# Routing of the expert layers: look-up in PSUM, exponential on VectorE, ScalarE loop of eight tiles

## The chip, the cores and the metric

The kernel runs on one core of a Trainium2 chip. Its engines are TensorE (PE in the rows, its weight loads PEld), VectorE (DVE), ScalarE (ACT), GpSimd (POOL) and SyncE (SP), which issues the DMAs. The metric is the device time of one execution in microseconds.

## The reference

256 tokens of width 1024 pass a two-layer block (gated linear attention, then sliding-window attention) and a second block with a mixture of experts. Each of the first two layers ends in `peer`, product-key retrieval over 128 x 128 experts of one neuron each, and only that is touched here:

```
s1, s2  = scores of the two query halves against 128 subkeys each, for 8 heads
v1, i1  = top_k(s1, 16);  v2, i2 = top_k(s2, 16)
cand    = v1[..., :, None] + v2[..., None, :]            # 16 x 16 sums
cs, ci  = top_k(cand, 16)
e       = take(i1, ci // 16) * 128 + take(i2, ci % 16)   # the expert picked
g       = softmax(cs)
a       = gelu(x . u_tab[e]);   y = sum over picks of g * a * v_tab[e]
```

## The kernel before

The kernel doesn't gather experts. It multiplies all tokens by the whole first table (`peer_u`, 16384 rows), keeps the GELU of every product in `W`, builds from the picks a table of gates by one-hot products, multiplies `W` by it, and multiplies the result by the whole second table. All of it is in fp32: each table tile of 128 x 1024 is split in a high and a low part, and each product is three matmuls (high x high, high x low, low x high).

The first-table stage has 128 tiles per layer. A tile is two halves of 512 columns, and there are four half buffers `w_parts`. For each half:

- SyncE loads the tile to one of four `ring` slots when TensorE has begun a later tile (`ring_free`).
- ScalarE copies the half to its high part (`high`, L1404) when TensorE has released the buffer (`half_free`).
- GpSimd subtracts it from the tile to get the low part (L2460).
- TensorE issues 12 matmuls of 256 columns (L952), so 24 per tile, into bank 0, 1, 2 or 3.
- After the second half ScalarE stores the GELU of the bank in `W` (`gelu`, L1409).

Each engine's program is written out in order. The loops are hardware loops (`Fori`). ScalarE's loop before the change holds four tiles, in the order `high(i+2)`, `gelu(i)`, and it runs in three parts: tiles 0 to 35, 36 to 71, 72 to 123. At the start of the second and the third part ScalarE takes one exponential (L1421) that VectorE has asked for (`cs`) and answers by `ecs`.

Beside this stage VectorE does the routing (`peer_dve`), for two token tiles of 128 tokens one after the other (the loop over `a`): top 16 of each score row (MAX8, FIND_INDEX8, MATCH_REPLACE8, L1964 to L1977), the 16 x 16 sums (L1989), their top 16 (L1996 to L2009), then the look-up. That compares the rank of each pick with 0 to 15 (L2031), multiplies by the indices (L2034) and adds up (L2037), each on 2048 columns in SBUF, once for each query half. Last come the sum of the exponentials and the division (L2040 to L2044), for which VectorE waits for ScalarE's exponential.

When tile 71 is done, TensorE turns the picks of the two token tiles with three transposes each (L905). They need a bank of 0 to 3, so TensorE waits first for the GELU of tile 71 (`gelu`) and for `picked`. VectorE copies each turned tile to `route` (L2050). TensorE starts tile 72, and ScalarE its third part, when both copies are done; the arena of `W` from tile 72 on lies over the routing's buffers.

## Time and profile before

| what | us |
|---|---|
| median of three runs | 3252.25 (3243.31 to 3254.04) |
| the profiled execution | 3245.69 |
| its span | 3243.9 |
| TensorE busy | 2985.8 (92%) |
| VectorE busy | 1982.0 (61%) |
| ScalarE busy | 1762.6 (54%) |
| GpSimd busy | 1583.7 (49%) |

The span is from the first to the last instruction that was profiled. Busy shares are means over stages that are bound by different engines. In the chain of waits that ended last TensorE has 66% of the span, and ScalarE, GpSimd and VectorE have 9%, 8% and 6%. Matmul ends are modelled, so a matmul of 256 columns is shown with 0.28 us though the next one starts 0.12 us later.

### The profile page before, as it was taken

To read this page: it belongs to the slowest core of one execution; us is meant where nothing else is said; L and a number is where in the kernel's file an instruction comes from. 1 tells how busy PE (TensorE), PEld (TensorE's weight loads), DVE (VectorE), ACT (ScalarE), POOL (GpSimd) and SP (SyncE) were. 2 spreads that over 40 slices of the span, in tenths; PEclk is the share of its full clock that TensorE was granted. 3 is DMA by queue.
4 is the path that set the end of the run, shared out by engine and by line. 5 is a ranking of instruction groups with operands and counts; after the bars stand their busy time and mean duration, and the time that the engine had idled before them with its cause. 6 is when DMAs were issued, how large, how long until landed. Compare 5 with 4: busy or idle time off the path is not lost.

```text
span 3243.9 us, 57950 instructions
## 1 busy us (share of the span) xinstructions
PE 2985.8 (92%) x18908; PEld 2694.4 (83%) x18908; DVE 1982.0 (61%) x3234; ACT 1762.6 (54%) x3309; POOL 1583.7 (49%) x1229
## 2 busy tenths in 40 slices
PE   7988999987999986999999789999889999999998
PEld 6678999976787875899999667888789789999997
DVE  6647370047888868272600678888684436777776
ACT  1124777788555553367767875555554315555554
POOL 5867998875444436149988645444261011000100
PEclk8989999999999997999999989999999999999998
DMA  6544555520766643345555127666464235555553
GB/s 250 200 154 166 170 170 166 183 94 32 257 228 226 229 143 118 100 161 169 168 168 181 52 84 255 233 229 214 138 220 158 95 117 190 193 191 191 200 192 125
DMA packets 153461, 552.55 MB, mean 170 GB/s; under 512 B 16896, under 2 KB 19712, under 8 KB 153232
## 3 DMA queue, kind: packets, MB, share of 16 engines
q1 hardware_dynamic: 151136, 547.42, 49.8%
q10 hardware_dynamic: 2224, 3.87, 0.4%
q8 instruction: 53, 0.87, 0.1%
q14 instruction: 48, 0.39, 0.0%
HBM read 550.17 MB, written 1.05 MB: 170 GB/s over the span
## 4 chain that ended last, share of the span: by engine, by line
PE 66%; issue 9%; ACT 9%; POOL 8%; DVE 6%; DMA 1%; ACTq 0%; POOLq 0%; DVEq 0%; SPq 0%
PE bank L978 20%; PE bank L952 15%; PE bank L1223 11%; PE bank L747 6%; PE bank L1244 5%; ACT hT L1444 5%; POOL w_parts L2460 5%; PE bank L695 3%; ACT hT L1440 2%; POOL arena L2504 1%; DVE w_parts L1756 1%; POOL arena L2506 1%; POOL arena L2508 1%; DMA arena<-stream 1%; DMA ring<-stream 0%
## 5 line engine op out<-in xcount | busy, mean ns | idle before, releaser
L2460 POOL TENSOR_TENSOR w_parts<-ring,w_parts 128x512 fp32r<-128x512 f32 x512 | 686.0, 1366 | 180.1 <-ACT w_parts L1404 175.3
L952 PE MATMUL bank<-h_parts,w_parts 128*128 128x256 f32 x6144 | 745.6, 284 | 25.3 <-POOL w_parts L2460 23.3
L952 PEld LDWEIGHTS bank<-h_parts,w_parts 128*128 128x128 f32 x6144 | 741.3, 193 | 29.7 <-POOL w_parts L2460 27.2
L2504 POOL TENSOR_TENSOR arena<-arena,cact 128x1024 f32<-128x1024 f32 x80 | 166.9, 2086 | 742.0 <-DMA arena<-stream 741.9
L1404 ACT ACTIVATE w_parts<-ring 128x512 fp32r<-128x512 f32 x512 | 321.5, 630 | 204.1 <-PE bank L952 200.0
L1596 ACT ACTIVATE w_parts<-ring 128x512 fp32r<-128x512 f32 x384 | 242.0, 631 | 266.0 <-PE bank L1223 168.5
L1223 PEld LDWEIGHTS bank<-h_parts,w_parts 128*128 128x128 f32 x3072 | 374.2, 193 | 3.8 <-DVE arena L2322 1.5
L1223 PE MATMUL bank<-h_parts,w_parts 128*128 128x256 f32 x3072 | 375.1, 284 | 1.4 <-DVE arena L2322 1.4
L978 PE MATMUL bank<-w_parts,a_parts 128*128 128x512 f32 x1536 | 370.8, 397 | 1.2 <-DVE a_parts L2107 1.2
L978 PE MATMUL bank<-h_parts,a_parts 128*128 128x512 f32 x1536 | 365.0, 393 | 6.0 <-DVE a_parts L2107 5.9
L2391 DVE TENSOR_TENSOR w_parts<-ring,w_parts 128x512 fp32r<-128x512 f32 x376 | 271.1, 732 | 149.0 <-ACT w_parts L1596 145.7
L978 PEld LDWEIGHTS bank<-h_parts,a_parts 128*128 128x128 f32 x1536 | 284.9, 188 | 79.0 <-DVE a_parts L2107 20.8
L978 PEld LDWEIGHTS bank<-w_parts,a_parts 128*128 128x128 f32 x1536 | 286.8, 190 | 60.3 <-DVE a_parts L2107 2.0
L1463 ACT ACTIVATE a_parts<-arena 128x256 fp32r (+1 forms) x256 | 107.1, 418 | 363.9 <-PE bank L978 362.0
L695 PE MATMUL bank<-h_parts,w_parts 128*128 128x256 f32 x1920 | 240.6, 287 | 15.2 <-DVE w_parts L1756 13.2
L695 PEld LDWEIGHTS bank<-h_parts,w_parts 128*128 128x128 f32 x1920 | 236.3, 195 | 18.9 <-issue 14.6
L2107 DVE TENSOR_TENSOR a_parts<-arena,a_parts 128x256 fp32r<-128x256 f32 x256 | 164.9, 644 | 123.2 <-ACT a_parts L1463 123.0
L1756 DVE TENSOR_TENSOR w_parts<-ring,w_parts 128x512 fp32r<-128x512 f32 x184 | 196.5, 1100 | 60.8 <-ACT w_parts L1297 59.5
L926 PE MATMUL bank<-hT,h_parts 128*128 128x128 f32 x1024 | 146.0, 295 | 68.8 <-ACT hT L1444 66.2
L2065 DVE COPY bank<-cst 128x128 f32<-128x128 f32 x2 | 0.6, 295 | 326.8 <-ACT arena L1409 326.8
L926 PEld LDWEIGHTS bank<-hT,h_parts 128*128 128x128 f32 x1024 | 129.1, 202 | 85.7 <-ACT hT L1444 85.4
L1244 PE MATMUL bank<-w_parts,a_parts 128*128 128x512 f32 x768 | 182.1, 393 | 6.0 <-DVE a_parts L2403 5.1
(325 smaller groups left out, 4661.7 us busy)
## 6 DMA issues: line engine op xcount, KB each, us to landing
ring<-stream SPq DMA_DIRECT2D x786, 512.0 KB, 3.4
arena<-stream SPq DMA_DIRECT2D x192, 512.0 KB, 4.3
hT<-stream SPq DMA_DIRECT2D x32, 512.0 KB, 4.6
mean<-stream SPq DMA_DIRECT2D x32, 512.0 KB, 4.6
arena<-consts ACTq DMA_DIRECT2D x1, 1536.0 KB, 6.9
xT<-xin ACTq DMA_DIRECT2D x1, 1024.0 KB, 10.8
out<-hT SPq DMA_DIRECT2D x4, 256.0 KB, 2.2
arena<-subk ACTq DMA_DIRECT2D x2, 128.0 KB, 2.2
```

Of the source, the lines that this page charges most:

```text
L695: mm = pe.matmul(t[:, 0:T], w[:, wp, q * P:(q + 1) * P], h_parts[:, hp, 4 * j + q, :], start=(j == 0 and q == 0 and i == 0), stop=(j == 1 ...
L926: mm = pe.matmul(bank[4 + k][:, (s % 4) * P:(s % 4 + 1) * P], hot2[:, s, :].bitcast(F32), hot1[:, s, :], start=True, stop=True)
L952: mm = pe.matmul(bank[k][:, 0:T], w[:, wp, ws], h_parts[:, hp, 4 * j + q, :], start=(j == 0 and q == 0 and i == 0), stop=(j == 1 and q == ...
L978: mm = pe.matmul(bank[4 + 2 * a + e][:, :], a_parts[:, k % 2, ap, a * P:(a + 1) * P], w[:, wp, :], start=False, stop=False, skip_group_che ...
L1223: mm = pe.matmul(bank[2 * e_par + m][:, f * T:(f + 1) * T], w[:, wp, q * P:(q + 1) * P], h_parts[:, hp, 4 * j + q, :], start=(j == 0 and q ...
L1244: mm = pe.matmul(bank[4 + 2 * a + e][:, :], a_parts[:, ap, f, a * P:(a + 1) * P], w[:, wp, :], start=(f == 0 and i == 0), stop=(f == 1 and ...
L1404: act.activation(w_parts[half % HALVES][:, 0, :], ring[slot_][:, j * 512:(j + 1) * 512], ACT.Copy).then_inc(sem(f"{n}_high"), 1)
L1596: act.activation(w_parts[half % HALVES][:, 0, :], ring[s][:, j * 512:(j + 1) * 512], ACT.Copy).then_inc(sem("e_high"), 1)
L1756: dve.tensor_tensor(w[:, 1, :], slot(name, k)[:, j * 512:(j + 1) * 512], w[:, 0, :].bitcast(F32), ALU.subtract).then_inc(sem("x_low"), 1)
L2391: dve.tensor_tensor(w[:, 1, :], ring[moe_slot(k)[0]][:, j * 512:(j + 1) * 512], w[:, 0, :].bitcast(F32), ALU.subtract).then_inc(sem("e_low ...
L2460: pool.tensor_tensor(w[:, 1, :], ring[(base + k) % RING][:, j * 512:(j + 1) * 512], w[:, 0, :].bitcast(F32), ALU.subtract).then_inc(sem(f" ...
L2504: pool.tensor_tensor(b3, b3, c_b, ALU.mult).then_inc(sem("mod_step"), 1)
```

## The change

It touches the first-table stage of both `peer` layers.

- VectorE's look-up works on 512 columns (two heads) at a time, in the PSUM banks 4, 5 and 6, which no matmul uses in this stage. The numbers 0 to 15 and a copy of the top values (`values_p`) lie in bank 7, so that each two-input operation of the sums and of the look-up reads one input from PSUM and one from SBUF.
- The exponential is made by VectorE with `exp_dve`, a series of order 8, on 128 columns in SBUF. The semaphores `cs` and `ecs` are gone, and VectorE does both token tiles without waiting for ScalarE.
- The picks are turned in banks 4 and 5. TensorE waits for `picked` alone, and goes on to tile 72 without waiting for VectorE's copies. ScalarE's second part waits for `picked` alone too.
- ScalarE's loop holds eight tiles, in the order `gelu(i)`, `high(i+3)`, with three `high` ahead of it. It has two parts, tiles 0 to 71 and 72 to 119, and eight tiles behind them.

```
-            pe.wait_ge(sem(f"{n}_gelu"), ROUTE_TILE)
+            pe.wait_ge(sem(f"{n}_picked"), TT)
             for a in range(TT):
-                ... wait for picked, open a tile of banks 0 to 3, wait till it is free
                 for k in range(3):
-                    mm = pe.transpose(t[:, k * P:(k + 1) * P], R.pick[:, a, k, :], ident)
-                mm.then_inc(full_sem(f"{n}_rt{a}"), 1)
-            for a in range(TT):
-                pe.wait_ge(free_sem(f"{n}_rt{a}"), freed(f"{n}_rt{a}"))
+                    mm = pe.transpose(bank[4 + a][:, k * P:(k + 1) * P], R.pick[:, a, k, :], ident)
+                mm.then_inc(sem(f"{n}_turned"), 1)
...
-            for i in range(2):
+            for i in range(3):
                 high(i, 2 * i, tile_at(i), base)
-            for part, (first, last) in enumerate(((0, 36), (36, 72), (72, NK - 4))):
-                ... from the second part on: wait for cs, Exp, then ecs
-                with act.Fori(first // 4, last // 4) as it:
-                    for k in range(4):
-                        high((k + 2) % 4, ...)
-                        gelu(bass.ds(it * 4 + k, 1), k, ...)
+            for first, last in ((0, ROUTE_TILE), (ROUTE_TILE, NK - 8)):
+                if first:
+                    act.wait_ge(sem(f"{n}_picked"), TT)
+                with act.Fori(first // 8, last // 8) as it:
+                    for k in range(8):
+                        gelu(bass.ds(it * 8 + k, 1), k % 4, it * 16 + 2 * (k + 1))
+                        high((k + 3) % 8, it * 16 + 2 * (k + 3), it * 32 + tile_at(k + 3), base)
...
+                dve.tensor_copy(values_p, v)
                 dve.tensor_tensor(c4, v4[:, :, 0, :]...,
-                                             v4[:, :, 1, :]..., ALU.add)
+                                             p4[:, :, 1, :]..., ALU.add)
...
+                dve.tensor_scalar(cs, cs, -87.0, None, ALU.max)
+                exp_dve(dve, weights, cs, R.ca, R.cb)
...
+                for f, rank in enumerate((R.caf, R.cbf)):
+                    for i in range(PH // 2):
+                        wide = bank[4 + i % 3][:, :]
+                        dve.tensor_tensor(w4, rank3[...], iota16[...], ALU.is_equal)
+                        dve.tensor_tensor(w4, w4, i4[:, hs, f, :]..., ALU.mult)
+                        dve.tensor_reduce(R.pick[:, a, f, ...], wide..., AX.X, ALU.add)
-                dve.wait_ge(sem(f"{n}_ecs"), a + 1)
```

`exp_dve(dst, x, tmp, tmp2)` was there and is called anew. Each line below waits for the one before it:

```
k = tensor_scalar(x * 1/ln2)        # rounded to int, in tmp
tmp2 = tensor_copy(k)
x = scalar_tensor_tensor(tmp2 * -LN2_HI + x);  x = scalar_tensor_tensor(tmp2 * -LN2_LO + x)
k = tensor_scalar(tmp2 + 127);  k = tensor_scalar(k << 23)
dst = tensor_scalar(x * c[8])
for i in 7..1: dst = scalar_tensor_tensor((dst + c[i]) * x)
dst = scalar_tensor_tensor((dst + 1) * tmp)
```

ScalarE, the start of the first loop of the stage, before. `arena<-bank` is a GELU, `w_parts<-ring` half a `high`, ISA and REGISTER_ALU handle waits and counts.

```order
L1403 ISA
L1404 ACT_TABLE_LOAD
L1404 ACTIVATE w_parts<-ring 128x512
L1403 REGISTER_ALU
L1404 ACTIVATE w_parts<-ring 128x512
L1409 ISA
L1409 ACT_TABLE_LOAD
L1409 ACTIVATE arena<-bank 128x256
L1399 REGISTER_ALU
L1403 REGISTER_ALU
L1404 ACTIVATE w_parts<-ring 128x512
L1403 REGISTER_ALU
```

And of the changed kernel:

```order
L1404 ISA
L1404 ACT_TABLE_LOAD
L1404 ACTIVATE arena<-bank 128x256
L1394 ISA
L1398 REGISTER_ALU
L1399 ACTIVATE w_parts<-ring 128x512
L1398 REGISTER_ALU
L1399 ACTIVATE w_parts<-ring 128x512
L1404 ISA
L1404 ACTIVATE arena<-bank 128x256
L1398 REGISTER_ALU
L1399 ACTIVATE w_parts<-ring 128x512
```

Before, the body of four tiles has two table loads, one for each kind of activation; now the body of eight tiles has one, ahead of the first GELU, and the second loop has none.

TensorE, the end of tile 71 and the turn, before, with the semaphores that a row waits for:

```order
L942 COMPARE_AND_BRANCH
L905 MATMUL bank<-cst,arena 128x128 [waits bank_free3,p0_picked,p0_gelu]
L905 MATMUL bank<-cst,arena 128x128 x2
L905 MATMUL bank<-cst,arena 128x128 [waits bank_free0,p0_picked]
L905 MATMUL bank<-cst,arena 128x128 x2
L942 UNCONDITIONAL_BRANCH [waits bank_free0,bank_free3]
L942 ISA
L952 MATMUL bank<-h_parts,w_parts 128x256 [waits p0_low]
```

And of the changed kernel:

```order
L937 COMPARE_AND_BRANCH
L902 MATMUL bank<-cst,arena 128x128 [waits p0_picked]
L902 MATMUL bank<-cst,arena 128x128 x5
L937 UNCONDITIONAL_BRANCH
L937 ISA
L947 MATMUL bank<-h_parts,w_parts 128x256 [waits p0_low]
```

The waits for `gelu`, for free banks between the transposes, and on the branch into the next loop are gone; the six transposes stand in one row.

VectorE, the look-up of a token tile and what closes it, before:

```order
L2025 CAST arena<-arena 128x128
L2031 TENSOR_TENSOR arena<-arena,cst 128x2048
L2034 TENSOR_TENSOR arena<-arena 128x2048
L2037 TENSOR_REDUCE arena<-arena 128x128
L2031 TENSOR_TENSOR arena<-arena,cst 128x2048
L2034 TENSOR_TENSOR arena<-arena 128x2048
L2037 TENSOR_REDUCE arena<-arena 128x128
L2040 TENSOR_REDUCE arena<-arena 128x8
L2042 RECIPROCAL arena<-arena 128x8
```

Of the changed kernel, first what is new ahead of it (L1841 to L1861 are `exp_dve`):

```order
L2014 TENSOR_SCALAR arena<-arena 128x128
L1841 TENSOR_SCALAR arena<-arena 128x128
L1843 CAST arena<-arena 128x128
L1845 SCALAR_TENSOR_TENSOR arena<-arena 128x128
L1847 SCALAR_TENSOR_TENSOR arena<-arena 128x128
L1849 TENSOR_SCALAR arena<-arena 128x128
L1851 TENSOR_SCALAR arena<-arena 128x128
L1856 TENSOR_SCALAR arena<-arena 128x128
L1859 SCALAR_TENSOR_TENSOR arena<-arena 128x128 x7
```

then the first two of the eight rounds of the look-up:

```order
L2024 CAST arena<-arena 128x128
L2032 TENSOR_TENSOR bank<-arena,bank 128x512
L2036 TENSOR_TENSOR bank<-bank,arena 128x512
L2039 TENSOR_REDUCE arena<-bank 128x32
L2032 TENSOR_TENSOR bank<-arena,bank 128x512
L2036 TENSOR_TENSOR bank<-bank,arena 128x512
L2039 TENSOR_REDUCE arena<-bank 128x32
```

The two rounds of three operations on 2048 columns in SBUF have become eight rounds of three on 512 columns with PSUM operands, and 16 operations on 128 columns have come in ahead of them.

## Rows read from the trace of the kernel before

**Rows 1.** The page's costliest groups: shape, count, busy us, mean ns, idle before

```profile
L2460 POOL TENSOR_TENSOR w_parts<-ring,w_parts 128x512 fp32r<-128x512 f32 x512 | 686.0, 1366 | 180.1 <-ACT w_parts L1404 175.3
L952 PE MATMUL bank<-h_parts,w_parts 128*128 128x256 f32 x6144 | 745.6, 284 | 25.3 <-POOL w_parts L2460 23.3
```

**Rows 2.** Windows view, both first-table stages: length, busy us (count), clock, DMA

```profile
302.70:689.50 386.80, 373.74 (x3078) 371.33 (x3078) 117.88 (x366) 276.39 (x446) 343.60 (x257) 1.00 0.53 174
1419.20:1806.10 386.90, 373.64 (x3078) 371.12 (x3078) 118.13 (x368) 276.37 (x446) 342.97 (x257) 1.00 0.53 174
```

**Rows 3.** Windows view, a stretch without VectorE work

```profile
530.00:689.00 159.00, 159.00 (x1326) 159.00 (x1326) 0.00 (x0) 114.95 (x188) 138.64 (x110) 1.00 0.56 182
```

**Rows 4.** Timeline of ScalarE, one loop turn: start, us, engine, line

```profile
369.62 1.28 ACT L1409 ACT_TABLE_LOAD   x1
381.14 1.28 ACT L1409 ACT_TABLE_LOAD   x1
```

**Rows 5.** Waits of TensorE, 302.7:510 and 1419.2:1630: total us, times, longest

```profile
PE bank L952 <- POOL w_parts L2460: 11.6, 9, 2.5
...
PE bank L952 <- POOL w_parts L2460: 11.8, 10, 2.5
```

**Rows 6.** L2460 on GpSimd in 302.7:315.2, 347.8:355, 334:340: ns min/median/max

```profile
L2460 POOL TENSOR_TENSOR w_parts<-ring,w_parts x11: 1293/1302/1308, 302.6 to 315.2; 128x512 fp32r<-128x512 f32 x11
...
L2460 POOL TENSOR_TENSOR w_parts<-ring,w_parts x4: 1286/2304/3312, 346.6 to 352.4; 128x512 fp32r<-128x512 f32 x4
...
L2460 POOL TENSOR_TENSOR w_parts<-ring,w_parts x5: 1292/1294/1342, 333.1 to 338.2; 128x512 fp32r<-128x512 f32 x5
```

**Rows 7.** Timeline, first look-up of layer 0 (start us, us, instruction, idle before)

```profile
339.90 2.29 DVE L2031 TENSOR_TENSOR arena<-arena,cst 128x2048 f32<-128x2048 f32 x1
...
342.23 3.27 DVE L2034 TENSOR_TENSOR arena<-arena 128x2048 f32<-128x2048 f32 x1
...
345.53 2.29 DVE L2037 TENSOR_REDUCE arena<-arena 128x128 f32<-128x2048 f32 x1
...
346.67 2.54 PE L952 MATMUL bank<-h_parts,w_parts 128*128 128x256 f32 x19 [1.57 <-POOL w_parts L2460]
```

**Rows 8.** Timeline, 128-column VectorE operations beside GpSimd

```profile
334.43 1.34 DVE L2015 TENSOR_TENSOR arena<-arena 128x128 f32<-128x128 f32 x1
...
335.80 1.20 DVE L2019 TENSOR_SCALAR arena<-arena 128x128 uint32<-128x128 uint32 x1
```

**Rows 9.** L2470 on GpSimd and L2072 on VectorE, whole program: ns min/median/max

```profile
L2470 POOL TENSOR_TENSOR hT<-cst,mean x128: 1039/1042/1044, 687.9 to 1907.2; 128x512 f32<-128x512 f32 x128
...
L2072 DVE TENSOR_TENSOR h_parts<-bank,mean x128: 680/683/692, 690.8 to 1907.8; 128x512 fp32r<-128x512 f32 x128
```

**Rows 10.** Timeline, the turn after tile 71 of layer 0

```profile
522.59 0.55 PE L905 MATMUL bank<-cst,arena 128*128 128x128 f32 x3 [0.99 <-ACT arena L1409]
...
524.81 0.29 DVE L2044 TENSOR_TENSOR arena<-arena 128x128 f32<-128x128 f32 x1
...
525.16 0.55 PE L905 MATMUL bank<-cst,arena 128*128 128x128 f32 x3 [2.03 <-DVE arena L2044]
...
526.68 1.28 ACT L1404 ACT_TABLE_LOAD   x1 [2.53 <-DVE mean L2050]
...
526.70 1.14 PE L952 MATMUL bank<-h_parts,w_parts 128*128 128x256 f32 x4 [1.00 <-DVE mean L2050]
```

**Rows 11.** Windows view of L952, just behind the turn (PE, PEld, PEclk, DMA)

```profile
526.70:530.00 3.30, 3.30 (x16) 3.30 (x17) 0.52 0.50 160
```

**Rows 12.** Timeline of VectorE: ends of the two token tiles, layer 0

```profile
292.73 0.49 DVE L1964 MAX8 arena<-arena 128x8 f32<-128x128 f32 x2 [1.37 <-ACT arena L1343]
...
354.57 2.29 DVE L2037 TENSOR_REDUCE arena<-arena 128x128 f32<-128x2048 f32 x1
414.80 0.29 DVE L2040 TENSOR_REDUCE arena<-arena 128x8 f32<-128x128 f32 x1 [57.94 <-ACT arena L1421]
...
475.56 2.29 DVE L2037 TENSOR_REDUCE arena<-arena 128x128 f32<-128x2048 f32 x1
```

More of the change, by code:

```diff
@@ L1412, in tile_at @@
                 return 16 * ((base + i) // RING + 1)
-            for i in range(2):
+            for i in range(3):
                 high(i, 2 * i, tile_at(i), base)
-            for part, (first, last) in enumerate(((0, ROUTE_TILE // 2), (ROUTE_TILE // 2, ROUTE_TILE), (ROUTE_TILE, NK - 4))):
-                if part:
-                    act.wait_ge(sem(f"{n}_cs"), part)
-                    act.activation(R.cs, R.cs, ACT.Exp).then_inc(sem(f"{n}_ecs"), 1)
-                if part == 2:
-                    for a in range(TT):
-                        act.wait_ge(free_sem(f"{n}_rt{a}"), freed(f"{n}_rt{a}"))
-                with act.Fori(first // 4, last // 4) as it:
-                    for k in range(4):
-                        high((k + 2) % 4, it * 8 + 2 * (k + 2), it * 16 + tile_at(k + 2), base)
-                        gelu(bass.ds(it * 4 + k, 1), k, it * 8 + 2 * (k + 1))
-            for i in range(NK - 4, NK):
-                if i + 2 < NK:
-                    high((i + 2) % 4, 2 * (i + 2), tile_at(i + 2), base)
+            for first, last in ((0, ROUTE_TILE), (ROUTE_TILE, NK - 8)):
[5 more added lines that the diff above has]
+                        high((k + 3) % 8, it * 16 + 2 * (k + 3), it * 32 + tile_at(k + 3), base)
+            for i in range(NK - 8, NK):
                 gelu(slice(i, i + 1), i % 4, 2 * (i + 1))
+                if i + 3 < NK:
+                    high((i + 3) % 8, 2 * (i + 3), tile_at(i + 3), base)
             act.wait_ge(sem(f"{n}_negated"), 1)
@@ L2015, in peer_dve @@
                 dve.tensor_tensor(R.cs, R.cs, R.sum[:, 0:8].unsqueeze(2).broadcast_to([P, PH, TOPK]),
-                                            ALU.subtract).then_inc(signal(f"{n}_cs"), 1)
-                dve.wait_ge(sem(f"{n}_cs"), signalled(f"{n}_cs"))
+                                            ALU.subtract).then_inc(signal("dve_step"), 1)
+                dve.wait_ge(sem("dve_step"), signalled("dve_step"))
+                weights = R.pick[:, a, 2, :]
+                cs = R.cs.rearrange("p h k -> p (h k)")
+                dve.tensor_scalar(cs, cs, -87.0, None, ALU.max).then_inc(signal("dve_step"), 1)
+                dve.wait_ge(sem("dve_step"), signalled("dve_step"))
+                exp_dve(dve, weights, cs, R.ca, R.cb)
                 cif = R.ci.rearrange("p h k -> p (h k)").bitcast(U32)
@@ L2039, in peer_dve @@
-                dve.wait_ge(sem(f"{n}_ecs"), a + 1)
-                dve.tensor_reduce(R.sum[:, 0:8], R.cs, AX.X, ALU.add).then_inc(signal("dve_step"), 1)
+                for f, rank in enumerate((R.caf, R.cbf)):
+                    rank3 = rank.rearrange("p (h k) -> p h k", h=PH)
+                    for i in range(PH // 2):
+                        hs = slice(2 * i, 2 * i + 2)
+                        wide = bank[4 + i % 3][:, :]
+                        w4 = wide.rearrange("p (h k x) -> p h k x", h=2, k=TOPK)
+                        dve.tensor_tensor(w4, rank3[:, hs, :].unsqueeze(3).broadcast_to([P, 2, TOPK, TOPK]),
+                                          iota16.unsqueeze(1).unsqueeze(1).broadcast_to([P, 2, TOPK, TOPK]), ALU.is_equal)\
+                           .then_inc(signal("dve_step"), 1)
+                        dve.wait_ge(sem("dve_step"), signalled("dve_step"))
+                        dve.tensor_tensor(w4, w4, i4[:, hs, f, :].unsqueeze(2).broadcast_to([P, 2, TOPK, TOPK]), ALU.mult)\
+                           .then_inc(signal("dve_step"), 1)
+                        dve.wait_ge(sem("dve_step"), signalled("dve_step"))
+                        dve.tensor_reduce(R.pick[:, a, f, 2 * i * TOPK:(2 * i + 2) * TOPK],
+                                          wide.rearrange("p (k x) -> p k x", x=TOPK), AX.X, ALU.add).then_inc(signal("dve_step"), 1)
+                        dve.wait_ge(sem("dve_step"), signalled("dve_step"))
@@ L2041, in peer_dve @@
+                w3 = weights.rearrange("p (h k) -> p h k", h=PH)
+                dve.tensor_reduce(R.sum[:, 0:8], w3, AX.X, ALU.add).then_inc(signal("dve_step"), 1)
                 dve.wait_ge(sem("dve_step"), signalled("dve_step"))
@@ L2461, in peer_pool @@
                                            w[:, 0, :].bitcast(F32), ALU.subtract).then_inc(sem(f"{n}_low"), 1)
-            for a in range(TT):
-                pool.wait_ge(free_sem(f"{n}_rt{a}"), freed(f"{n}_rt{a}"))
+            pool.wait_ge(sem(f"{n}_route"), TT)
             with pool.Fori(0, T // TURN) as it:
```

35 lines of the change are left out of this document (12 added, 23 removed).

## The prediction

> **What bounds the kernel now.** I read the page first. The costliest group on GpSimd and the costliest on TensorE belong to one stage, the first-table stage, and each waits for the other's chain: TensorE lost 23.3 us to GpSimd there [rows 1]. So the windows view comes next. Each of the two stages takes 386.8 to 386.9 us [rows 2]. A stretch without VectorE work shows what it could take: TensorE is busy without a gap, 1326 matmuls in 159.00 us, 0.12 us each [rows 3], and ScalarE's table load comes again after 11.52 us per four tiles [rows 4], which is 96 x 0.12. So 128 tiles at TensorE's own pace are 32 x 11.52 = 368.6 us, and each stage loses 18.2 us. Two table loads per four tiles are already inside this pace: they cost TensorE nothing while GpSimd is undisturbed.
>
> The waits view gives the largest part: TensorE waited 11.6 us for L2460 in layer 0 before the turn, 11.8 us in layer 1 [rows 5]. Why, the durations of L2460 tell: 1.30 us undisturbed, up to 3.31 us beside the look-up [rows 6]. The timeline says beside which operations: the two-input ones on 2048 columns in SBUF (L2031, L2034), which take 2.29 us, or 3.3 us when they have first to wait for GpSimd. Behind L2034 TensorE stood 1.57 us [rows 7]. L2037, a reduction with one input, takes 2.29 us at any time. So VectorE and GpSimd keep each other out of SBUF when VectorE reads two inputs there.
>
> The rest is the turn after tile 71. The last matmul of the tile, shown as 0.28 us, starts 0.99 + 0.28 us ahead of 522.59, at 521.32, and the first of tile 72 at 526.70 [rows 10]. At full pace it would have come 0.12 us later, so 5.3 us are lost: waits of 0.99, 2.03 and 1.00 us and two times three transposes. Then 16 matmuls took 3.30 us where 27.5 would have fitted, at a granted clock of 0.52, the lower of its two levels, after TensorE had stood nearly still [rows 11]: 11.5 x 0.12 = 1.4 us. 11.6 + 5.3 + 1.4 = 18.3 us, which closes with 18.2.
>
> **Part by part.** *The look-up and the sums in PSUM.* The trace of before has this form of operation beside GpSimd in the next stage: L2072 reads one input from PSUM and one from SBUF, 512 columns, and takes 0.680 to 0.692 us in 128 cases, while GpSimd's L2470, which runs beside it, takes 1.039 to 1.044 us in all 128 [rows 9]. Neither touches the other. So L2460 stays at 1.30 us and the waits of rows 5 go: 11.6 + 11.8 = 23.4 us. The bounds are 23.4 gained and, if a PSUM operand did not help, a loss that the second rival works out. I take 23.4, since rows 9 is the same form at the same width. For VectorE a look-up is then 16 x 0.68 plus 8 reductions of a quarter of 2.29, or 15.5 us, near what it took.
>
> *The exponential on VectorE.* 16 new operations on 128 columns in SBUF per token tile. Beside GpSimd such operations took 1.34 and 1.20 us [rows 8], alone 0.29 (L2044 in rows 10): they wait for the end of a GpSimd operation. I take 1.25 us, so 20 us per token tile. What they do to GpSimd is in the third of rows 6: five L2460 beside them took 1.292 to 1.342 us. Two of at most 1.34 us are 2.68 us per tile, and TensorE needs 2.88 us for a tile, so it stays ahead. Cost 0. The other bound: each keeps GpSimd out for its own 0.29 us, 4.6 us per token tile, of which GpSimd's spare time in 20 us (7 tiles x 0.28) takes 2.0. That leaves 2.6 us, four times 10.4 us in the program.
>
> The Trainium skill speaks against this part: "SBUF — State Buffer", section "Who interferes with whom", says that a VectorE instruction with two SBUF inputs, or a copy or tensor_scalar in a two-port mode, blocks GpSimd for the whole instruction. On the long operations rows 7 agrees. On the short ones GpSimd's worst case was 0.05 us longer, so by the rule the sum would be the other bound, by the trace it is 0, and I keep the trace.
>
> *No wait for ScalarE.* VectorE's first token tile took from 292.73 to 356.9 us; then it stood 57.94 us until ScalarE's exponential, and ended the second look-up at 477.9 [rows 12]. Now it goes through: 292.7 + (64 + 20) + 1 + (62 + 20) = about 460 us. TensorE is at the turn at 302.7 + 72 x 2.88 = 510. So the picks are ready 50 us ahead, and the added `picked` waits of TensorE and ScalarE, behind which every later tile is queued, find it fulfilled. ScalarE's stop for the two exponentials (one table load and 0.31 us each) goes; TensorE hardly felt the first, and the second is in the turn.
>
> *The turn.* What is left is six transposes, starting some 0.11 us apart (three are shown as 0.55 with the last one's tail), and the restart of the loop; after the wait ended TensorE needed about 0.3 us. Together 0.7 + 0.3 + 0.1 = 1.1 us where 5.3 were. The stop is then too short to take the clock down: behind waits of 1.6 us [rows 7] matmuls came at full pace. So 4.2 + 1.4 = 5.6 us per layer, 11.2 in all. Bounds: 0.7 to 2.5 us for the new turn, and the clock's 1.4 lost again. What is late next is nothing: GpSimd and ScalarE work on during the transposes and fill all four half buffers.
>
> *ScalarE's loop.* One table load per eight tiles, none behind tile 71, where it was two per four. The order of `high` and `gelu` stays the same in effect (three ahead and GELU first is the same row of instructions as two ahead and `high` first). The loads were hidden in rows 3, so their absence is worth 0; it gives GpSimd more spare time, which covers the exponential. Worth at most the 0.4 us per layer at the first exponential, already counted.
>
> *The stages behind* have the same instructions, and the first of them starts when the last GELU is stored.
>
> Sum: 23.4 + 11.2 = 34.6 us; I leave 0.6 us for gaps that stay, so 34 us. On the profiled execution, 3245.7 us, that gives 3211.7. It lies 6.6 us below the median of the three runs; the four executions together have a mean of 3248.8, and from there it is 3215 us, which I give.
>
> **The rivals.** *The small operations block GpSimd for their own length.* For it: they do wait for GpSimd, so they do share something. Against it: the 0.05 us. It costs 10.4 us: 3225. It is what the rule above would give.
>
> *A PSUM operand does not free GpSimd's port.* Then 16 operations of 0.68 us hold GpSimd off per token tile, 10.9 us; before, four did for 2.0 us each, 8.1, and TensorE lost about 5.7 of it (a quarter of 23.4, near enough), so 2.4 are cushion. Now it loses 8.5, and four times 2.8 us more than before are 11 us, as much as the turn gives: no change, 3249. Rows 9 speak against it.
>
> *The gain is given back behind.* The next stage or the loads are late by themselves. The 16 DMA engines are busy for 0.56 even at full pace [rows 3], and the next stage waits on nothing but engines. If half were given back: 3232.
>
> *Slower: the picks come late.* TensorE now meets `picked` without any cover. If VectorE ends the second token tile behind 510 us, every microsecond is TensorE's, in both layers. It decides from 510 + 17 = 527 us, 67 us later than my 460. That needs each of the 48 look-up operations per layer to wait for one GpSimd operation (1.3 us), 62 us, and a little more. If the small ones also waited for two instead of one (32 x 1.3 = 42 us), VectorE would end at 564, TensorE would lose 54 us per layer, and the time would be 3215 + 108 = 3323. In rows 9 no such wait is seen.
>
> **Chances.** Forecast 0.78 (3205 to 3224 with the spread of runs, 3243 to 3254 before), small operations block 0.09, given back 0.05, port not freed 0.05, late picks 0.02, anything else 0.01. The range is 3202 to 3230: it takes in the first rival and leaves out the others, some 0.13, and little at the low end. A measurement of this kernel tells 0.3%, 10 us, from no change. Faster by more than that: 0.92 (the forecast, the first rival and the gain half given back); within it: 0.06; slower: 0.02.
>
> **What would show it.** Right: L2460 at 1.3 us throughout both stages, none above 1.4; no wait of TensorE for it; each first-table stage 370 us long; TensorE's stop at the turn near 1 us with the granted clock at full level behind it; VectorE through with both token tiles near 460 us with no wait for ScalarE; one table load per eight tiles. Wrong: L2460 at 1.9 us beside the look-up, or regularly above 1.4 beside the series; a stop of TensorE at the turn that VectorE ends; a later stage that is longer than before.

## The result, and the profile after

The changed kernel takes 3216.39 us (median of four runs, 3211.73 to 3217.48), the kernel before 3249.55 us (four runs, 3243.31 to 3254.04). The ratio is 0.9896, with a 95% interval of 0.9883 to 0.9909: 33 us less, 30 to 38. The forecast was 3215, with a range of 3202 to 3230. The profiled execution took 3215.80 us, its span is 3214.0 us.

The windows view of the changed kernel, over both first-table stages (length, then busy us and count of PE, PEld, DVE, ACT, POOL, then clock, DMA share, GB/s), answers to [rows 2]:

```profile
303.90:673.20 369.30, 369.29 (x3078) 369.29 (x3078) 148.49 (x436) 205.73 (x389) 331.25 (x257) 1.00 0.56 182
1403.50:1772.80 369.30, 369.29 (x3078) 369.30 (x3078) 148.50 (x436) 205.74 (x389) 331.13 (x257) 1.00 0.56 182
```

386.8 us have become 369.3 us, in both layers, and TensorE is busy in all of it. Its own pace for 128 tiles is 368.6 us. The two stages together are 35.0 us shorter.

The waits view of TensorE in 303.9:512, against [rows 5] (total us, times, longest):

```profile
PE bank L947 <- POOL w_parts L2462: 2.5, 1, 2.5
```

This one wait ends at 303.9, where the stage's first matmul starts: it lies ahead of the stage, and no wait within the stage is left. The longest wait of [rows 5], 2.5 us, is the same one in the kernel before, so it never was part of what the stage lost.

GpSimd's subtraction over the whole program (ns min/median/max), which was up to 3.31 us beside the look-up in [rows 6]:

```profile
L2462 POOL TENSOR_TENSOR w_parts<-ring,w_parts x512: 1267/1297/1422, 302.6 to 1768.1; 128x512 fp32r<-128x512 f32 x171
```

None is longer than 1.42 us. What VectorE does beside it, from the timeline of layer 0 (start, us, instruction), answers to [rows 7, 8]:

```profile
315.80 2.29 DVE L1985 TENSOR_TENSOR arena<-arena,bank 128x2048 f32<-128x2048 f32 x1
...
345.27 10.04 DVE L1859 SCALAR_TENSOR_TENSOR arena<-arena 128x128 f32<-128x128 f32 x7
...
355.35 0.29 DVE L1861 SCALAR_TENSOR_TENSOR arena<-arena 128x128 f32<-128x128 f32 x1
...
358.77 0.69 DVE L2032 TENSOR_TENSOR bank<-arena,bank 128x512 f32<-128x512 f32 x1
359.50 0.70 DVE L2036 TENSOR_TENSOR bank<-bank,arena 128x512 f32<-128x512 f32 x1
360.23 0.69 DVE L2039 TENSOR_REDUCE arena<-bank 128x32 f32<-128x512 f32 x1
```

The sums with one PSUM input take 2.29 us, where they took 3.27 to 3.36 with both in SBUF. The look-up's three operations take 0.69 to 0.70 us each, with no wait among them. Seven operations of the series take 10.04 us, one every 1.43 us, and the last one, which met GpSimd idle, 0.29. GpSimd's subtractions beside these seven start every 1.44 us, which is TensorE's own pace for half a tile, and last 1.29 to 1.30 us.

The turn after tile 71 in the changed kernel, against [rows 10], then the windows view of the matmuls just behind it, against [rows 11]:

```profile
511.37 0.82 PE L902 MATMUL bank<-cst,arena 128*128 128x128 f32 x6
...
511.94 4.32 PE L947 MATMUL bank<-h_parts,w_parts 128*128 128x256 f32 x34
511.96 1.02 DVE L2052 COPY mean<-bank 128x384 f32<-128x384 f32 x2 [57.24 <-PE bank L902]
```

```profile
511.90:515.20 3.30, 3.26 (x27) 3.29 (x28) 1.00 0.51 155
```

The six transposes take 0.57 us from their start to tile 72's, and 27 matmuls follow in 3.30 us at the full clock, where before there were 16. The wait of 57.24 us at VectorE's copy says that the picks had been ready since 454.7 us. ScalarE's table loads of layer 0 up to there, from the view by lines:

```profile
L1404 ACT ACT_TABLE_LOAD x9 | 11.5, 1283 | 0.2
```

They were 37 in the same stretch, one of them for the exponential.

### The profile page after: what moved, and what is told of

The parts are those of the page before. It is cut to its first block, busy times and chain, and to the rows that moved or that the text cites. A ratio compares the mean times of both kernels' runs of the same rounds, so it can differ in the third digit from the quotient of the medians.

```text
span 3214.0 us, 57845 instructions
## 1 busy us (share of the span) xinstructions
PE 2985.8 (93%) x18908; PEld 2696.5 (84%) x18908; DVE 2045.3 (64%) x3376; ACT 1621.4 (50%) x3195; POOL 1562.5 (49%) x1229
## 4 chain that ended last, share of the span: by engine, by line
PE 74%; ACT 9%; DVE 6%; issue 6%; POOL 3%; DMA 1%; ACTq 0%; DVEq 0%; SPq 0%; POOLq 0%
PE bank L947 23%; PE bank L973 20%; PE bank L1218 12%; PE bank L747 6%; PE bank L1239 5%; ACT hT L1434 5%; PE bank L695 3%; ACT hT L1430 2%; POOL arena L2505 1%; DVE w_parts L1746 1%; POOL arena L2507 1%; PE bank L649 1%; DMA arena<-stream 1%; POOL arena L2509 1%; DMA ring<-stream 1%
## 5 line engine op out<-in xcount | busy, mean ns | idle before, releaser
L2462 POOL TENSOR_TENSOR w_parts<-ring,w_parts 128x512 fp32r<-128x512 f32 x512 | 661.9, 1300 | 169.9 <-ACT w_parts L1399 119.3
L947 PE MATMUL bank<-h_parts,w_parts 128*128 128x256 f32 x6144 | 738.3, 283 | 5.1 <-POOL w_parts L2462 5.1
L947 PEld LDWEIGHTS bank<-h_parts,w_parts 128*128 128x128 f32 x6144 | 737.5, 191 | 5.5 <-POOL w_parts L2462 5.5
L973 PEld LDWEIGHTS bank<-h_parts,a_parts 128*128 128x128 f32 x1536 | 284.7, 188 | 80.4 <-DVE a_parts L2109 22.4
## 6 DMA issues: line engine op xcount, KB each, us to landing
xT<-xin ACTq DMA_DIRECT2D x1, 1024.0 KB, 10.7
```

The lines of the kernel that those rows point to most:

```text
L947: mm = pe.matmul(bank[k][:, 0:T], w[:, wp, ws], h_parts[:, hp, 4 * j + q, :], start=(j == 0 and q == 0 and i == 0), stop=(j == 1 and q == ...
L973: mm = pe.matmul(bank[4 + 2 * a + e][:, :], a_parts[:, k % 2, ap, a * P:(a + 1) * P], w[:, wp, :], start=False, stop=False, skip_group_che ...
L2462: pool.tensor_tensor(w[:, 1, :], ring[(base + k) % RING][:, j * 512:(j + 1) * 512], w[:, 0, :].bitcast(F32), ALU.subtract).then_inc(sem(f" ...
```

## The experiments

A stage's length is from the first to the last of its 3072 matmuls, read from the view by source line; it varies less from run to run than the time of the whole program. Differences of stages are taken before rounding. "By the starts of the matmuls" means how much later than 0.12 us one starts after the other, added up over a stretch. Times of different runs are compared by their ratio to the kernel before on the same chip.

| kernel | stage, layer 0 and 1, us | ratio to before (95%) | median us |
|---|---|---|---|
| before | 386.8, 386.8 | 1 | 3249.6 |
| changed | 369.3, 369.3 | 0.9896 (0.9883 to 0.9909) | 3216.4 |
| PSUM operands alone | 376.6, 375.9 | 0.9930 (0.9913 to 0.9947) | 3223.8 |
| series and turn alone | 381.3, 381.5 | 0.9974 (0.9962 to 0.9987) | 3238.4 |
| turn alone | 384.6, 386.1 | 0.9998 (0.9988 to 1.0008) | 3247.5 |
| loop of eight alone | 387.1, 386.6 | 0.9994 (0.9980 to 1.0007) | 3250.7 |
| changed, look-up in SBUF | 380.9, 380.0 | 0.9954 (0.9937 to 0.9970) | 3232.9 |
| changed, 512-column look-up in SBUF | 375.0, 374.9 | 0.9931 (0.9911 to 0.9951) | 3226.9 |
| changed, comparison from SBUF | 369.3, 369.3 | one run, no interval | 3207.2 |
| changed, sums from SBUF | 369.3, 369.3 | one run, no interval | 3206.9 |
| changed, loop of four | 369.3, 369.3 | 0.9891 (0.9866 to 0.9916) | 3215.4 |
| changed, series twice | 369.3, 369.3 | 0.9886 (0.9870 to 0.9903) | 3214.5 |
| changed, loop of four and sums from SBUF | 369.4, 369.4 | 0.9906 (0.9889 to 0.9922) | 3220.0 |
| changed, late picks | 398.1, 399.3 | 1.0072 (1.0055 to 1.0089) | 3273.6 |

### The look-up alone, forward and back

PSUM operands alone: the kernel before, with

```
-            iota16 = iota[:, 0:TOPK]
+            iota16 = bank[7][:, 0:TOPK]
+            values_p = bank[7][:, TOPK:TOPK + 256]...
...
+                dve.tensor_copy(values_p, v)      # and the sums and the look-up as in the change
```

> The kernel before with one part of the change alone: sums and look-up with PSUM operands; exponential on ScalarE, the turn in banks 0 to 3 and the loop of four as before. My theory: each first-table stage lasts 386.8 - 11.7 = 375.1 us and the time is 23 us below the kernel before, 3227. Rival (the parts only work together, since two table loads per four tiles leave GpSimd no spare time): a stage above 380 us and a gain below 12 us.

Measured: 0.9930, 23 us less. The first matmul and the last of each layer, and GpSimd's subtraction over the whole program:

```profile
L952 PE MATMUL bank<-h_parts,w_parts x3072: 278/283/577, 302.1 to 678.8; 128*128 128x256 f32 x192
...
L952 PE MATMUL bank<-h_parts,w_parts x3072: 278/283/416, 1408.7 to 1784.7; 128*128 128x256 f32 x192
```

```profile
L2470 POOL TENSOR_TENSOR w_parts<-ring,w_parts x512: 1266/1293/1395, 300.8 to 1779.9; 128x512 fp32r<-128x512 f32 x171
```

376.6 and 375.9 us against 375.1 expected, and no subtraction above 1.40 us. Two table loads per four tiles did not keep the gain away. What is left above 368.6 us, 7.3 to 8.0 us, is 0.4 us at the first exponential and the old turn: counted from the starts of the matmuls, a stop of 5.3 to 5.7 us, and 1.6 to 1.9 us by which the next 60 matmuls came late.

The other way round, the changed kernel with

```
-                for f, rank in enumerate((R.caf, R.cbf)):      # eight rounds of 512 columns in PSUM
+                for f, (rank, wide) in enumerate(((R.caf, R.cand), (R.cbf, R.cand2))):   # 2048 columns in SBUF, as before
```

> The changed kernel with one part undone: the look-up works again on 2048 columns in SBUF. My theory (a second SBUF input of VectorE holds GpSimd off; a PSUM input frees it): L2460's successor goes up to 3.3 us again, TensorE loses about 5.5 us per token tile, each first-table stage lasts 369.3 + 11 = 380 us instead of 369.3, and the time is 22 us above the changed kernel's, 3238. Rival (it is ScalarE's spare time, from fewer table loads, that took the stalls in): the stages stay under 373 us and the time under 3224.

```profile
L947 PE MATMUL bank<-h_parts,w_parts x3072: 277/283/579, 303.4 to 684.3; 128*128 128x256 f32 x192
...
L947 PE MATMUL bank<-h_parts,w_parts x3072: 278/283/388, 1416.9 to 1796.8; 128*128 128x256 f32 x192
```

```profile
L2458 POOL TENSOR_TENSOR w_parts<-ring,w_parts x512: 1267/1297/3437, 302.0 to 1792.1; 128x512 fp32r<-128x512 f32 x171
```

Measured: 380.9 and 380.0 us, 380 expected, and subtractions of up to 3.44 us are back. In layer 0, 1.2 us of this belong to the first 12 matmuls of the stage, which met the clock at its lower level (0.50 in 303.4:306.0, where the changed kernel had 1.00 in 303.9:306.5), and not to the look-up. The time rose by less than the 22 us that I gave: the ratio went from 0.9896 to 0.9954, 19 us, with intervals that leave 9 to 28. The rival (fewer table loads would take the stalls in) asked for stages under 373 us and falls.

### Is it the place or the size of the pieces?

The change did two things to the look-up at once: PSUM operands and pieces of 512 columns. So the pieces alone:

```
-                        wide = bank[4 + i % 3][:, :]
+                        wide = R.cand2...[:, (i % 3) * 512:(i % 3 + 1) * 512]     # SBUF
-                          iota16...                                               # bank 7
+                          iota[:, 0:TOPK]...                                      # SBUF
```

> The changed kernel with its look-up in the same eight rounds of 512 columns, but all of it in SBUF (three pieces in turn, numbers 0 to 15 from SBUF). It tells the place of the operands from the size of the pieces. My theory (the second SBUF input): each of the 16 two-input operations per token tile takes turns with GpSimd, so one L2462 lasts 1.3 + 0.6 us, 3.8 us per tile where TensorE needs 2.88; over the eight tiles that pass TensorE loses about 5 us after the cushion, in each token tile: a first-table stage of 379 to 381 us and a time 20 us above the changed kernel's, 3237. Rival (short pieces are enough, since four half buffers take each in): a stage under 371 us and the changed kernel's time.

```profile
L947 PE MATMUL bank<-h_parts,w_parts x3072: 277/283/388, 305.2 to 680.2; 128*128 128x256 f32 x192
```

```profile
L2462 POOL TENSOR_TENSOR w_parts<-ring,w_parts x512: 1266/1297/1769, 303.9 to 1781.8; 128x512 fp32r<-128x512 f32 x171
...
L2036 DVE TENSOR_TENSOR arena<-arena x32: 692/1670/1681, 361.8 to 1581.4; 128x512 f32<-128x512 f32 x32
```

Measured: 375 us, between the two theories. GpSimd's subtraction reaches 1.77 us beside the pieces, 0.47 more and not my 0.6, and VectorE's multiplication takes 1.67 us: in the timeline it starts while a subtraction runs and ends 0.55 us behind it. TensorE then waits often and briefly (some 20 waits of its weight loads in layer 0), and a stage loses 5.7 us where 2048 columns lost 11. So small pieces would have brought about half of the look-up's gain; PSUM brings the other half. The loss that I gave for this run, 10 to 12 us per stage, was twice too high.

Then which operand counts, the input or the output? Only the comparison, one operation in three, with both inputs from SBUF and its output in PSUM as in the change:

```
-                          iota16.unsqueeze(1)...          # bank 7
+                          iota[:, 0:TOPK].unsqueeze(1)... # SBUF
```

> The changed kernel with both inputs of the look-up's comparison (8 of 24 operations per token tile, 512 columns) in SBUF, its output still in PSUM. It tells whether the second SBUF input or the SBUF output counts. My theory (the input): the comparison takes up to 2 us instead of 0.70 when it has to wait, GpSimd's operations reach 1.9 us beside it, eight times per token tile, and TensorE loses nothing or up to 1 us per token tile, since the other two thirds leave GpSimd time to catch up. Rival (the output): the comparison stays at 0.70 and GpSimd at 1.3 us.

```profile
L2032 DVE TENSOR_TENSOR bank<-arena,cst x32: 699/1466/1689, 359.8 to 1562.6; 128x512 f32<-128x512 f32 x32
...
L2462 POOL TENSOR_TENSOR w_parts<-ring,w_parts x512: 1270/1297/1822, 303.6 to 1765.8; 128x512 fp32r<-128x512 f32 x171
...
L2036 DVE TENSOR_TENSOR bank<-bank,arena x32: 698/699/700, 361.5 to 1564.1; 128x512 f32<-128x512 f32 x32
```

The comparison rises from 0.70 to as much as 1.69 us and GpSimd's operations beside it to 1.82 us, while the multiplication right behind it, which has one SBUF input, stays at 0.70 in all 32 cases. The output was in PSUM throughout, so it is the second SBUF input. The other way round, the changed kernel's sums write 2048 columns to SBUF with one SBUF input, take 2.29 us in all four cases, and no subtraction goes above 1.42 us. The stage stays at 369.3 us: one such piece in three is taken in.

### The series and the turn

Series and turn alone: the kernel before with the exponential on VectorE and the turn in banks 4 and 5, but look-up, sums and loop as before.

> The kernel before with the exponential on VectorE and the turn in banks 4 and 5, but the look-up and the sums in SBUF and the loop of four. My theory: the turn costs TensorE 0.7 us instead of 5.3 and the clock stays up (6 us per layer), and 0.4 us at the first exponential goes: each first-table stage 386.8 - 6.4 = 380.4 us, the time 12 to 13 us below the kernel before, 3237. Rival (the 16 small operations of the series per token tile take GpSimd's time where two table loads per four tiles leave it none): 2.6 us per token tile back, a stage of 385 us or more, a gain of 2 to 4 us.

```profile
L947 PE MATMUL bank<-h_parts,w_parts x3072: 274/283/387, 304.4 to 685.7; 128*128 128x256 f32 x192
...
L947 PE MATMUL bank<-h_parts,w_parts x3072: 278/283/388, 1410.9 to 1792.4; 128*128 128x256 f32 x192
```

Measured: 381.3 and 381.5 us against 380.4 expected (the rival: 385 or more), and 0.9974, 8 us less, 4 to 12. The stages are 0.9 to 1.1 us longer than I gave. By the starts of the matmuls TensorE lost 0.75 us in each layer beside the second token tile's sums, which cost it nothing in the kernel before, and 0.45 us more beside the two look-ups.

The two halves alone gave 21.0 and 10.7 us of stage, 31.7 together, and both at once 35.0. Of the missing 3.3 us, 2.4 are these losses, which the runs with PSUM operands do not have. The rest is the turn of the run with PSUM operands alone, which was 0.7 and 0.2 us slower than that of the kernel before.

The turn without the series: the kernel before with

```
-            pe.wait_ge(sem(f"{n}_gelu"), ROUTE_TILE)
+            pe.wait_ge(sem(f"{n}_picked"), TT)      # banks 4 and 5, no wait for the copies
...                                                  # ScalarE's third part waits for picked too
```

> The kernel before with the turn alone changed: the picks are turned in banks 4 and 5, TensorE waits for both token tiles' picks and not for the GELU, and not for VectorE's copies; the exponential stays on ScalarE behind the GELU of tile 71. My theory (what the turn costs is above all the wait for the exponential): the picks are ready 3.7 us after the last matmul of tile 71, the transposes and restart add 0.7, so the stop is 4.4 us instead of 5.3 and the lower clock behind it stays: a stage of 386 us, the time 2 us below the kernel before, the same within the error. Rival (it is the waits for the banks and the copies): the stop falls to 1 us, a stage of 381 us, 11 us less.

The timeline of its turn in layer 0:

```profile
524.22 1.28 ACT L1416 ACT_TABLE_LOAD   x1
525.51 0.31 ACT L1416 ACTIVATE arena<-arena 128x128 f32<-128x128 f32 x1
...
525.92 0.29 DVE L2034 TENSOR_REDUCE arena<-arena 128x8 f32<-128x128 f32 x1 [46.42 <-ACT arena L1416]
...
526.83 0.88 PE L902 MATMUL bank<-cst,arena 128*128 128x128 f32 x6 [3.57 <-DVE arena L2038]
...
527.46 2.76 PE L947 MATMUL bank<-h_parts,w_parts 128*128 128x256 f32 x21
```

The time did not move (0.9998, 0.9988 to 1.0008). The stages are 2.2 and 0.7 us shorter, which this interval of 3 us either way can't tell from nothing. The transposes and the restart are nearly as short as in the change, 0.63 us against 0.57, but the picks come only at 526.8 us: ScalarE loads its table and takes the exponential behind the GELU of tile 71, and VectorE divides behind that. TensorE waits 3.57 us. So most of the turn's gain hangs on the series. What the series would bring with the old turn was not tried: how much of the 5.2 to 5.5 us per stage needs both is open. The windows behind this turn, layer 0 and layer 1, show something else:

```profile
527.40:530.70 3.30, 3.30 (x30) 3.30 (x29) 1.32 (x3) 1.63 (x3) 0.81 (x1) 1.00 0.46 160
1637.50:1640.80 3.30, 3.30 (x19) 3.30 (x18) 1.27 (x3) 1.41 (x2) 0.04 (x1) 0.55 0.46 159
```

Both stops were 4.36 us beyond the pace, and the granted clock behind them was full in layer 0 (27 of L947's matmuls in 3.30 us) and for most of the window at the lower level in layer 1 (17). The clock alone is worth 1.5 us between the two.

### What should cost nothing

Loop of eight alone: the kernel before with parts of 40, 32 and 48 tiles, eight in a turn. It keeps `high` first. With the GELU first and three `high` ahead, `high(74)` would stand in front of the exponential that TensorE's tile 72 needs, and neither could go on; that order can only be had with the series on VectorE.

```
-            for part, (first, last) in enumerate(((0, 36), (36, 72), (72, NK - 4))):
+            for part, (first, last) in enumerate(((0, 40), (40, 72), (72, NK - 8))):
-                with act.Fori(first // 4, last // 4) as it:
-                    for k in range(4):
+                with act.Fori(first // 8, last // 8) as it:
+                    for k in range(8):
```

> The kernel before with ScalarE's loop of eight tiles (parts of 40, 32 and 48 tiles), still high first and with the exponentials on ScalarE, so two table loads per eight tiles instead of four. My theory: the stalls beside the look-up are as long as GpSimd is held off, whatever ScalarE does, so each first-table stage stays at 386 to 387 us and the time is the same as before. Rival (the spare time takes stalls in): a stage of 382 to 384 us, 6 to 9 us less.

```profile
L952 PE MATMUL bank<-h_parts,w_parts x3072: 277/283/574, 303.8 to 690.9; 128*128 128x256 f32 x192
...
L952 PE MATMUL bank<-h_parts,w_parts x3072: 277/283/522, 1424.0 to 1810.6; 128*128 128x256 f32 x192
```

387.1 and 386.6 us and a ratio of 0.9994: in 303.8:520 ScalarE has 18 table loads beside the exponential's, where it had 36, and nothing is gained.

Loop of four in the changed kernel, `high` first:

```
-            for i in range(3):
+            for i in range(2):
...
-                with act.Fori(first // 8, last // 8) as it:     # gelu(i), high(i + 3)
+                with act.Fori(first // 4, last // 4) as it:     # high(i + 2), gelu(i)
```

> The changed kernel with ScalarE's loop of four tiles again, high first: two table loads per four tiles, all else as changed. My theory (the table loads are hidden): each first-table stage 369.3 to 370.5 us, the time that of the changed kernel, 3216. Rival (GpSimd has no spare time left for the 16 small operations of the series: 8 x 1.33 + 1.23 = 11.9 us where TensorE needs 11.52): about 1 to 2 us per token tile, a stage of 372 to 374 us.

Both stages are 369.3 us long, and the ratio is 0.9891 where the changed kernel has 0.9896. The table loads are hidden even beside the series.

The series twice:

```
+                    dve.tensor_copy(R.caf, cs)
+                    exp_dve(dve, R.cbf, R.caf, R.ca, R.cb)      # scratch
                 exp_dve(dve, weights, cs, R.ca, R.cb)
```

> The changed kernel with the series made once more per token tile on scratch columns: 16 more small operations in SBUF. My theory: they wait for GpSimd, 1.35 us each, and cost it under 0.1 us each, which its spare time takes in: VectorE ends the second token tile near 498 us of the span instead of 454.7, each first-table stage stays at 369.3 us, the time at 3216. Rival (each small operation holds GpSimd off for its own 0.3 us): 2 to 3 us per token tile, a stage of 374 us, 9 us more.

Both stages are 369.3 us long. VectorE's copy at the turn:

```profile
512.11 1.02 DVE L2056 COPY mean<-bank 128x384 f32<-128x384 f32 x2 [18.38 <-PE bank L902]
```

The wait shrank from 57.24 to 18.38 us: VectorE worked 39 us longer, and TensorE did not feel it. No subtraction goes above 1.42 us, as in the changed kernel. 16 small operations more per token tile cost nothing, and neither do the 16 of the change: its stages have only 0.6 to 0.7 us above TensorE's pace, and the turn takes 0.57 of them.

The sums from SBUF in the changed kernel:

```
-                                             p4[:, :, 1, :]..., ALU.add)
+                                             v4[:, :, 1, :]..., ALU.add)
```

> The changed kernel with both inputs of the 16 x 16 sums (2048 columns, once per token tile) in SBUF. My theory: one operation of GpSimd is stretched by up to 2 us, and the four half buffers are a cushion of about that length, as in the kernel before, where the sums cost TensorE nothing: each first-table stage 369.3 us, at most 369.8. Rival (every two-input operation in SBUF costs TensorE its length): 2 x 2 us more, a stage of 373 us.

```profile
L2462 POOL TENSOR_TENSOR w_parts<-ring,w_parts x512: 1272/1297/3331, 303.4 to 1765.4; 128x512 fp32r<-128x512 f32 x171
...
L1985 DVE TENSOR_TENSOR arena<-arena x4: 2802/2878/2941, 316.6 to 1494.5; 128x2048 f32<-128x2048 f32 x4
```

One subtraction per token tile is stretched, to 3.33 us, and the stages are 369.3 us all the same. One such stall is taken in; that it is the cushion of four half buffers that does it is argued from the program, not tried with fewer buffers.

Both together:

> The changed kernel without the two parts that cost nothing when taken back alone: ScalarE's loop of four tiles, high first, and the sums with both inputs in SBUF. What is left of the change is the look-up in PSUM, the series and the turn. My theory (each of the two has a cover: the cushion of four half buffers for the sums, TensorE's pace for the table loads): together they meet once or twice per stage, as in the run with the series and the turn alone, where TensorE stood 0.65 us beside the second sums; each first-table stage 369.3 to 370.0 us, the time the changed kernel's, 3216. Rival (they add up, since two table loads per four tiles leave GpSimd nothing to catch up with): a stage of 372 us or more, 6 us slower.

The stages are 369.4 us long, 0.15 to 0.18 us more than in the changed kernel, and the ratio is 0.9906 (0.9889 to 0.9922) against 0.9896 (0.9883 to 0.9909): no difference that can be told. The look-up in PSUM, the series and the turn are the change; the loop of eight and the copy of the values bring nothing that was measured. Two versions that ran once, the comparison and the sums from SBUF, took 3207.2 and 3206.9 us, below all four runs of the changed kernel. Their stages are not shorter: the difference lies outside them, and one run each can't tell it from spread. No version with an interval is faster than the changed kernel beyond it.

### The rival that forecast slower, priced

```
+                for again in range(56):
+                    dve.tensor_tensor(bank[4 + again % 3][:, :]..., bank[4 + again % 3][:, :]..., R.caf[:, 0:32]..., ALU.mult)
```

> The changed kernel with 56 multiplications on 512 columns in PSUM put into each token tile (on the scratch banks of the look-up, which nothing reads any more), 0.73 us each, so that VectorE ends the second token tile 82 us later. It puts a price on the rival that forecast slower. My theory: the end moves from 454.7 to 536.6 us, TensorE stands at the turn from 511.4 until then, 25 us, then 0.7 us and 1.4 us for the lower clock: each first-table stage 396 us instead of 369.3, the time 3216 + 54 = 3270, 20 us above the kernel before. Rival (ScalarE and GpSimd, which fill the half buffers meanwhile, give part back): less than 20 us per stage.

The turn in layer 0, and the windows view just behind it:

```profile
540.76 0.29 DVE L2053 TENSOR_TENSOR arena<-arena 128x128 f32<-128x128 f32 x1
...
541.10 1.54 PE L902 MATMUL bank<-cst,arena 128*128 128x128 f32 x6 [27.09 <-DVE arena L2053]
...
542.30 2.06 PE L947 MATMUL bank<-h_parts,w_parts 128*128 128x256 f32 x8
```

```profile
542.30:545.60 3.30, 3.30 (x21) 3.30 (x20) 1.22 (x3) 0.60 (x1) 0.00 (x0) 0.66 0.48 145
```

The picks came at 541.1 us, not 536.6, in part since this stage began 2.5 us later (306.4 against 303.9). TensorE stood 27.09 us. The stages are 398.1 and 399.3 us, 29 to 30 more than in the changed kernel, and the time is 0.72% above the kernel before. Nothing is given back: a late pick costs its own length, and the lower clock 1.1 us (layer 0) and 2.2 us (layer 1) on top, counted over the next 60 matmuls.

## Why the prediction was right

- *The stage and its bound.* I put each first-table stage at 368.6 us of TensorE's pace and 18.2 us of loss. It is 369.3 us now, so 17.5 of the 18.2 are gone.
- *The look-up, 23.4 us.* The cause is right, the size too large. The 11.6 and 11.8 us of [rows 5] each hold the wait of 2.5 us that ends where the stage begins, which the changed kernel still has. Without it the view has 9.0 and 9.3 us, and the starts of the matmuls show 10.8 and 11.1 us lost beside the look-ups, 21.9 in all. So it was in part luck that 11.6 + 5.3 + 1.4 closed with 18.2: with 10.8 it is 17.5, and the 0.4 us at the first exponential and 0.3 us of small terms are missing (the clock took 1.6 in layer 0, not 1.4). With PSUM operands alone the stages became 10.2 and 10.8 us shorter, 21.0, and the time fell by 23. Undone alone, it brought back 22.4 us of stage, 1.2 of them at the start of layer 0 and not by the look-up. The mechanism is shown from three sides: the long look-up in SBUF, the short one, and a single operation with its second input moved. The claim that it was the form of [rows 9] held: the comparison took 0.695 to 0.697 us and the multiplication 0.699 to 0.700.
- *The series, 0 us.* Right; twice the series cost nothing with PSUM operands. Beside a look-up and sums in SBUF (the run with the series and the turn alone) TensorE lost 1.2 us per stage more than in the kernel before; whether the series has a part in that was not tried apart. The rule of the Trainium skill's page "SBUF — State Buffer", section "Who interferes with whom", holds for the form of instruction (two SBUF inputs contend, one does not: the run with the comparison from SBUF shows just this), but a held GpSimd is not yet a lost microsecond: its spare 0.28 us per tile took in 32 operations per token tile. I had told the rule from one side only: the section gives the ports to whichever of the two starts first, and the other waits. Here the small operations of VectorE waited (up to 1.41 us for 0.29), and the 14 subtractions in 335.8:355.4 beside them had a median of 1.297 us and a longest of 1.354. I had 1.25 us per operation, 20 us per token tile; in layer 0 the 16 took 19.8 us in the first token tile, up to 1.41 each, and 15.9 us in the second, where several met GpSimd idle and took 0.29.
- *VectorE's end near 460 us.* 454.7. The reductions took 0.69 us, not the 0.57 that a quarter of the long one gives. This is not PSUM's doing: from SBUF, in the run with the pieces there, they took 0.685 to 0.690. A part of an operation's time does not shrink with its columns. But the sums lost their wait and some small operations found GpSimd idle.
- *The turn, 5.6 us per layer.* The stop was 0.57 us beyond the pace, where I gave 1.1, and the clock stayed up. By the starts of the matmuls the turn cost 6.9 us in layer 0 and 6.6 in layer 1 before and costs 0.6 to 0.7 now, so it brought 6.0 to 6.2 us per layer, where I gave 5.6. The parts of the 35.0 us are then 21.9 (look-up), 12.2 (turn) and 0.9 (first exponential), where I had 23.4, 11.2 and nothing apart: two errors of 1.5 and 1.9 us cancelled, and that the sum came this close is in part luck. The series and the turn together alone brought 5.2 to 5.5 us per stage.
- *ScalarE's loop, 0 us.* Right in both directions, alone and taken back.
- *The stages behind, 0 us.* The two stages gave 35.0 us, the medians 33.2. Outside the two stages the profiled execution of before took 2470 us and that of the changed kernel 2475. In the run with the sums from SBUF, whose code there is the same, it was 2466. In all 14 profiles it lies between 2466 and 2478 us, in the kernel before 2470. So this difference is within the spread between executions and no sign of a cost of the change; I can't say more than that from these runs.
- *The median from the mean of four executions* (3248.8 less 34) came within 2 us of the measured 3216.4. From the median, 3218, it would have been as close; from the profiled one, 3212, it would not. This is less than the spread of the runs and says nothing for the choice.

Of the rivals, *small operations block GpSimd for their own length* falls by the series made twice, *a PSUM operand does not free the port* by the look-up alone, and *late picks* did not occur, with a margin of 57 us where I had 50. Its price was right in kind: I had it decide at 527 us, 224 us into the stage. In the late run the picks came 541.1 - 306.4 = 235 us into it and the stage was 11.3 us longer than before, which puts the point at 223 us.

## What to carry to other kernels

When VectorE and GpSimd work at the same time and GpSimd feeds the bound engine, count VectorE's operations with two SBUF inputs and their length: here one long one cost nothing with four half buffers of cushion, four within 17 us cost about two thirds of the time by which they stretched GpSimd's work (5.5 of 8 us), and moving one input to PSUM ended it. Cutting them short got half. Take from a view of waits only those that lie within the stretch: the first row can be a wait that ends where it begins. A stop at a hand-over is only as short as its last producer: moving the hand-over to free banks alone gave 2.9 us of stage in the two layers together, about half of it by the clock, until the exponential was made early, elsewhere.

## What the runs showed of the hardware

- GpSimd's subtraction of 128 x 512 in SBUF (1.30 us) goes up to 3.31 to 3.44 us beside a VectorE operation with two SBUF inputs of 2048 columns, to 1.77 to 1.82 us beside 512 columns, and to no more than 1.42 us beside 128 columns. VectorE's own operation is stretched too: 0.29 us became up to 1.41, 0.70 became up to 1.69.
- The number of SBUF inputs decides, not where the output goes: VectorE's 512 columns took 0.699 to 1.689 us with two of them and a PSUM output, 0.698 to 0.700 us with one. With one SBUF input and an SBUF output, 2048 columns took 2.29 us four times.
- The granted clock behind a stop of TensorE: full behind 0.6 us, once full and once mostly at the lower level behind 4.4 us, and at the lower level for all or most of the next 3.3 us (0.50 to 0.66) behind 5.3 to 28 us. Behind these slow restarts 15 to 19 of the stage's matmuls started in 3.3 us instead of 27.5, and the first 60 matmuls came 1.1 to 2.2 us late.
- A reduction of 512 columns took 0.69 us from PSUM (0.691 to 0.692) and from SBUF (0.685 to 0.690) alike, and one of 2048 columns from SBUF 2.29.
